# Four experts instead of three on the two-pass 64-slot step, and a new order of the 56 expert steps

## The reference

```python
logits = (xt @ w_router).astype(jnp.float32)
top_val, top_idx = lax.top_k(logits, TOP_K)          # 2 of 8 experts
top_w = jax.nn.softmax(top_val, axis=-1)
gates = jnp.sum(jax.nn.one_hot(top_idx, N_EXPERTS) * top_w[..., None], axis=1)
for e in range(N_EXPERTS):
    y = y + gates[:, e:e + 1] * (silu(xt @ w_gate[e]) * (xt @ w_up[e])) @ w_down[e]
```

## Time and profile before

| | |
|---|---|
| three runs, median | 1363.91 us |
| lowest and highest | 1363.8 and 1367.77 us |
| span of the profiled execution | 1365.5 us |
| PE busy in it | 1331.8 us, 98% |
| DVE busy | 1107.3 us, 81% |
| ScalarE busy | 975.5 us, 71% |
| moved by DMA | 433.24 MB, 317 GB/s on the mean |

### The profile page before, as it was taken

One profiled execution on the slowest core, in us unless ns is written; L12 is line 12 of the kernel. 1 busy time (PEld: TensorE's weight loads), 2 busy tenths in 40 slices (PEclk: granted clock), 3 DMA queues, 4 the chain that ended last, 5 costly groups with the idle time before them and its releaser, 6 DMA issues.

```text
span 1365.5 us, 18288 instructions
## 1 busy us (share of the span) xinstructions
PE 1331.8 (98%) x7233; PEld 1123.6 (82%) x7233; DVE 1107.3 (81%) x885; ACT 975.5 (71%) x930; POOL 168.7 (12%) x103
## 2 busy tenths in 40 slices
PE   8989999999999999999999999999999999999996
PEld 7888999999999778777877888777877877787784
DVE  4664655555666599999999989999999999999995
ACT  5465544446556667888788878888888888878883
POOL 4251000000000132574400000000000000000001
PEclk8999999999999999999999999999999999999998
DMA  9305755554542389999999999999999999999992
GB/s 372 121 1 185 207 186 184 184 184 154 204 144 86 111 332 401 404 419 407 412 421 419 421 401 390 422 421 421 408 411 421 414 411 421 421 411 422 418 418 98
DMA packets 67203, 433.24 MB, mean 317 GB/s; under 512 B 8160, under 2 KB 10336, under 8 KB 18992
## 3 DMA queue, kind: packets, MB, share of 16 engines
q1 hardware_dynamic: 60320, 418.01, 76.4%
q0 software_dynamic: 3360, 12.22, 3.0%
q10 hardware_dynamic: 3440, 1.91, 0.8%
HBM read 426.09 MB, written 6.03 MB: 316 GB/s over the span
## 4 chain that ended last, share of the span: by engine, by line
PE 74%; DVE 11%; DMA 9%; ACT 4%; issue 1%; SPq 0%; DVEq 0%; ACTq 0%
PE banks L1887 21%; PE banks L1889 20%; PE banks L1888 20%; DMA raw<-in_moe_w_gate 9%; DVE w_lo L1169 6%; ACT w_hi L623 2%; PE banks L2451 2%; DVE qk_lo L1169 2%; PE banks L2120 2%; PE banks L2452 2%; ACT qk_hi L623 1%; PE banks L2108 1%; PE banks L2488 1%; PE banks L2490 1%; PE banks L2462 1%
## 5 line engine op out<-in xcount | busy, mean ns | idle before, releaser
L1169 DVE TENSOR_TENSOR w_lo<-raw,w_hi 128x2048 fp32r<-128x2048 f32 (+1 forms) x312 | 711.2, 2297 | 134.4 <-ACT w_hi L623 132.9
L623 ACT CAST w_hi<-raw 128x2048 fp32r<-128x2048 f32 (+1 forms) x312 | 592.5, 1909 | 161.8 <-PE banks L1889 125.5
L1169 DVE TENSOR_TENSOR qk_lo<-raw,qk_hi 128x2048 fp32r<-128x2048 f32 x84 | 192.0, 2286 | 13.0 <-ACT qk_hi L623 12.1
L623 ACT CAST qk_hi<-raw 128x2048 fp32r<-128x2048 f32 x84 | 160.0, 1905 | 14.3 <-PE banks L1889 9.5
L1887 PE MATMUL banks<-w_hi,t_hi 128*128 128x512 f32 (+2 forms) x444 | 164.7, 371 | 2.9 <-DVE w_lo L1169 1.5
L1889 PE MATMUL banks<-w_lo,t_hi 128*128 128x512 f32 (+2 forms) x444 | 161.6, 364 | 0.0
L1888 PE MATMUL banks<-w_hi,t_lo 128*128 128x512 f32 (+2 forms) x444 | 161.5, 364 | 0.0
L1887 PE MATMUL banks<-t_hi,w_hi 128*128 128x256 f32 x544 | 155.5, 286 | 0.9 <-DVE t_lo L1190 0.9
L1888 PE MATMUL banks<-t_hi,w_lo 128*128 128x256 f32 x544 | 154.3, 284 | 0.0
L1889 PE MATMUL banks<-t_lo,w_hi 128*128 128x256 f32 x544 | 154.2, 284 | 0.0
L1887 PE MATMUL banks<-w_hi,h_hi 128*128 128x512 f32 x300 | 118.8, 396 | 0.2 <-DVE w_lo L1169 0.2
(11 more groups left out here) (358 smaller groups left out, 2261.9 us busy)
## 6 DMA issues: line engine op xcount, KB each, us to landing
raw<-in_moe_w_gate SPq DMA_DIRECT2D x112, 1024.0 KB, 9.9
raw<-in_moe_w_up SPq DMA_DIRECT2D x112, 1024.0 KB, 9.3
raw<-in_moe_w_down SPq DMA_DIRECT2D x112, 1024.0 KB, 9.7
raw<-in_na_w_qkv SPq DMA_DIRECT2D x12, 1024.0 KB, 4.8
raw<-in_ffn_w_gate SPq DMA_DIRECT2D x11, 1024.0 KB, 5.0
raw<-in_ffn_w_up SPq DMA_DIRECT2D x11, 1024.0 KB, 5.1
raw<-in_ffn_w_down SPq DMA_DIRECT2D x11, 1024.0 KB, 4.9
raw<-in_w_in_e SPq DMA_DIRECT2D x6, 1024.0 KB, 15.7
```

What stands on the lines that cost most here:

```text
L623: act.copy(tile_hi(u, n), raw[:, u.raw, 0:n]).then_inc(hi_done, 1)
L1169: dve.tensor_tensor(tile_lo(u, n), raw[:, u.raw, 0:n], tile_hi(u, n).bitcast(F32), ALU.subtract).then_inc(lo_done, 1)
```

## The change

The step kinds are dealt out anew: positions 1, 3, 5 and 6 are small instead of 1, 4 and 6, so there are 28 big and 28 small steps instead of 35 and 21. The order of the steps is given by a string, in which each letter takes the next step of its kind, instead of by a list of big steps with small ones put behind some of them. `RANK_OF` follows: the four experts with the fewest tokens are small. The threshold in the sort goes from 2.5 to 3.5 (`len(SMALL_V) - 0.5`). `TURN_AT`, `SENT_AT` and `MOVE_AT` are computed from the order as before.

```diff
 SMALL = 64
-BIG_V, SMALL_V = (0, 2, 3, 5, 7), (1, 4, 6)
-SMALL_AFTER = ((3, 4, 5, 6, 8, 9, 10), (15, 16, 17, 18, 20, 21, 22), (24, 25, 26, 27, 29, 30, 31))
-RANK_OF = np.array([7, 2, 3, 4, 1, 5, 0, 6], np.float32)
+BIG_V, SMALL_V = (0, 2, 4, 7), (1, 3, 5, 6)
+PATTERN = "BBBBSBSBSSBBSSSBBSSSBBSSBSBSBBSSBSSSBSSBBSBSSBSBBSSBSBBB"
+RANK_OF = np.array([7, 3, 4, 2, 5, 1, 0, 6], np.float32)

 def step_order():

-    order = []
-    for m in range(MOE_STEPS * len(BIG_V)):
-        order.append((BIG_V[m // MOE_STEPS], m % MOE_STEPS))
-        for v, after in zip(SMALL_V, SMALL_AFTER):
-            if m in after:
-                order.append((v, after.index(m)))
+    order, taken = [], {"B": 0, "S": 0}
+    for kind in PATTERN:
+        m = taken[kind]
+        order.append(((BIG_V if kind == "B" else SMALL_V)[m // MOE_STEPS], m % MOE_STEPS))
+        taken[kind] += 1
     return order
...
-                dve.tensor_scalar(extra, rank, 2.5, float(SLOTS - SMALL), ALU.is_lt, ALU.mult).then_inc(sort_step, 1)
+                dve.tensor_scalar(extra, rank, len(SMALL_V) - 0.5, float(SLOTS - SMALL), ALU.is_lt, ALU.mult).then_inc(sort_step, 1)
```

## The result

The kernel after takes 1369.76 us (median of 20 runs, 1366.72 to 1373.81), the kernel before, in 20 runs beside it, 1367.17 us (1362.91 to 1370.58). The ratio is 1.0023 [1.0014, 1.0033]: 3.1 us slower by the ratio. That is under the 0.3% which the prediction took for the limit of what can be told, but on the other side of no change than the forecast of -0.8 us, and outside its range. The runs of each kernel lie in two groups some 4 us apart (before 1362.9 to 1365.0 and 1367.1 to 1370.6, after 1366.7 to 1368.7 and 1370.8 to 1373.8), and both groups lie higher after.

What follows compares the result with a forecast made beforehand. Weight transfers were taken to bound the expert stage at about 421 GB/s, so PE's 33.6 us less work gave 0 us and the smaller add -0.8 us: 1363.1 us from a median of 1363.91, range 1359.5 to 1367.0.

Steps and rivals of the forecast that it cites:

- The bound: Expert stage: weight transfers, full at about 421 GB/s, set the pace; 33.6 us less PE work gains 0 us.
- PE was the bound: Rival, expert stage: PE sets the pace, so all 33.6 us go, giving 1330 us; chance 0.06.
- the tally: Expert stage: PE's 846 us against the queue's 861; big steps add 2.0 us of lateness, small ones take 2.8 away.
- PE's idle time: Small steps of the expert stage: about 34 us more PE idle time, waiting for w_lo.
- One add of 64 instead of 96 rows: Adding an expert's rows back: one more small add takes 0.8 us less from the weight queue, range 0.6 to 1.3.
- The new order up to the tally: Steps from 9 on: at most two big steps in a row behind step 4, three at the end; lateness stays covered.
- Queues that are moved past: POOL's adds and gathers at new steps: tightest is step 40, 0 us; the other place is a rival.
- the rival behind it: POOL late with expert 7's pick table at step 14: PE could wait 5.6 us, giving 1369 us; chance 0.05.
- The table of step 14: Sign of a wrong prediction: step 14 waits for expert 7's pick table, which could take 22.3 us.
- the cover: Four split tiles hold 10 us of PE's lateness before the ring of weight buffers stands still.
- If the granted clock leaves 1.00: Sign of a wrong prediction, in a run of small steps: at 1.2 GHz one takes up to twice 12.1 us.
- step 40: POOL's add of expert 5, 7.8 us, then gather of 7, 8.7 us (at most 14.4), fit two steps, 29.9 us: 0 us.

Runs made afterwards that it cites:

- the first kernel: Kernel before, with half of each down load left out in the expert stage (two of a step's six loads at half length): 1363.07 us, ratio 0.9966.
- the second: Kernel after with slot work of positions 5 to 7 one to three steps later, and half of each down load left out: 1338.24 us, ratio 0.9791 to before.
- the later slots: Kernel after with PE's and VectorE's slot work of positions 5 to 7 one to three steps later: ratio to before 0.9990, repeated 0.9991.
- the old head: Kernel after with steps 8 to 10 again small, big, small and the new order behind them: ratio to before 0.9998.
- the run with VectorE's wait: Kernel after with VectorE waiting in step 8 until POOL's pick table of position 5 is set: ratio to before 1.0003.

## Why the prediction was right or wrong

*The bound: right.* The quiet stretch at the end still moves 420 GB/s, latency is 10.3 to 10.6 us, ScalarE's waits went from PE to the DMA, and what was taken from PE was worth next to nothing while the loads stood. None of the stretches read above shows the 435 or 439 GB/s that the rival "PE was the bound" needed; and of that rival's 33 us, 24 came out by the ratio, and only when the loads were cut as well. (In the stage it is 28.2, 813.3 against 1296.33 - 511.23 = 785.1, or an estimated 22 without the first kernel's stop. In the second PE is busy 98% of 508 to 1296 us and VectorE holds 24% of the chain, so some of the relief may be hidden there again.) One term of the tally was off. PE does not stand 15 us under the queue: with the loads cut the kernel before still needed 813.3 us from gather to add (1322.77 - 509.44) against 811.7 with them, and without its stop and the slow clock an estimated 807.6, so PE is within some 4 us of the queue. What of PE's work the three windows of the earlier trace rows leave out was not added up.

*PE's idle time: right in kind, less in size.* Forecast 34 us more; the busy time in the stage fell by 25 (808.94 to 783.91; the part at half clock counts as busy, at most 3.4 of it), and 4.8 of the 25 are the stop. With the later slots, without the stop, it is 789.60, 19 us less than before. What the rest is was not looked into.

*One add of 64 instead of 96 rows: not contradicted.* -0.8 us forecast; the stages of the later slots, their repeat and the old head are 0.7, 0.6 and 0.7 us shorter, and the queue loses 0.8, 1.1 and 1.0 us less. That fits, but it hangs on one profile of the kernel before, and nothing in it separates the add from the rest of the change. The total of a run cannot show it (0.9990 [0.9977, 1.0003]).

*The new order up to the tally: right.* Old head, new rest costs nothing that shows.

*"Queues that are moved past", and the rival behind it: here it failed.* The mechanism was the right one (a late pick table on POOL, PE's slot matmuls waiting for it at the head of a step, all its matmuls behind them), and the rival's 1369 us came within a microsecond of the result. That nearness is luck: the rival's 5.6 us stood on a base of 1363.91 and at step 14, while the loss is 3.1 us on a base of 1367.17 and at step 10. The table of step 14, the text's sign of being wrong, kept nobody waiting. The place and the cover were wrong, and so was the chance of 0.05. Three steps of the working failed:

1. The text says that up to step 8 the order is the old one, and then looks at where adds and gathers have moved, and so at step 14. It did not ask of each slot step whether its margin holds. Steps 9 and 10 changed places, and the slot matmuls of position 5 stand between them. The margin could be had from before: the table ended at 628.8, PE came at 633.9, 5.1 us. On the axis of before (the first copy of the table is 4.54 us earlier in after) PE now comes at 631.9, 2.0 us earlier, behind a small step.
2. The duration of a table was taken as a number (22.3 us at the worst). It is a wait for something on VectorE. With the steps swapped it ends, on the same axis, at 636.5, 7.7 us later. 2.0 + 7.7 - 5.1 = 4.6 us are the 4.76 that PE stands. Within them lies the other wait, for the low parts of the turned rows, which grew from 1.01 to 2.2 us; the text does not name it.
3. The cover of 10 us needs four tiles that ScalarE can still write while PE stands, and a PE at its full clock behind the wait. Neither held: ScalarE wrote one tile and then waited 8.43 us. It had already been waiting for PE in that stretch, before as after (4.1 us in five places before; 3.1 us in five places after, beside the stop), so all tiles but one were taken when the stop came. And the clock fell. "If the granted clock leaves 1.00" stood among the signs of a wrong prediction, but for runs of small steps, not for a single stop.

*The base.* The forecast stood on a median of three runs, 1363.91; the 20 beside the kernel after have 1367.17. So 3.3 us of the 6.7 between 1363.1 and 1369.76 are the base, and the other 3.4 are the step above. That the three runs came out low was bad luck. The text also sets the profile's span of 1365.5 us against a median of times; in the record the time of a run is 1.8 to 2.1 us longer than its span, so that execution lay about 3.4 us above the median, not 1.6. The forecast, 1363.91 - 0.8, does not depend on it. At step 40 it takes the shortest landings of the earlier trace rows, 7.8 and 8.7 us, for the usual ones, which are 9.3 and 9.4; the two steps' room covers these too.

## What to carry to other kernels

When an order is changed, go along each engine's waits and not along the moved work: for each wait ask how early its releaser was (the margin in the trace of before) and how much earlier the waiting engine now comes; here a margin of 5 us met an arrival 2 us earlier and a release 8 us later. When two resources are both full, relief for one shows nothing, and a kernel that cuts the other tells whether the relief is there. Read the profile of such a kernel as well: here it had a stop of its own. A stop of PE can cost more than its length, if the clock falls with it and the buffers are already taken; here dummy matmuls in the stop gave back about half to two thirds of the loss, but only where they began ahead of the stop.

## What the runs showed of the hardware

POOL's pick operation (128 x 96, one input from SBUF) takes 0.52 us in a pause of VectorE. Beside VectorE's back-to-back subtracts it ended after 2.47 or 4.97 us in some places, and did not end for 19.18, 21.85, 29.58 or 38.72 us in others: many of VectorE's instructions long, not one. In the kernel before it ended within a pause of 0.32 us on VectorE, at 628.78; in after VectorE has no such pause from 602.4 to the end at 631.97. That a pause lets it end is shown by the run with VectorE's wait, where it took 0.53 us.

```profile
623.99 4.48 DVE L1169 TENSOR_TENSOR w_lo<-raw,w_hi 128x2048 fp32r<-128x2048 f32 x2
628.79 2.29 DVE L1169 TENSOR_TENSOR w_lo<-raw,w_hi 128x2048 fp32r<-128x2048 f32 x1 [0.32 <-ACT w_hi L623]
```

```profile
626.05 0.74 DVE L1793 SCALAR_TENSOR_TENSOR arena<-banks,arena 64x512 f32<-64x512 f32 x1
626.71 2.28 DVE L1168 TENSOR_TENSOR qk_lo<-raw,qk_hi 128x2048 fp32r<-128x2048 f32 x1
628.91 0.55 DVE L1820 TENSOR_TENSOR kc_rest<-banks,kc_rest 128x384 fp32r<-128x384 f32 x1
629.38 2.28 DVE L1168 TENSOR_TENSOR w_lo<-raw,w_hi 128x2048 fp32r<-128x2048 f32 x1
631.58 0.42 DVE L1800 TENSOR_TENSOR h_hi<-banks,h_hi 128x256 fp32r<-128x256 f32 x1
```

The subtracts of L1168 read both inputs from SBUF. The Trainium skill (SBUF — State Buffer, section Who interferes with whom) says that such an instruction contends with a GpSimd instruction that reads SBUF, and that an instruction with at most one input from SBUF, outside the modes that use both ports, does not. The first agrees with these rows. The second does so in part: in after the table ended during L1800 (one input from the PSUM banks), but not during L1793 or L1820 ahead of it, which are of the same kind, nor during an earlier L1800 at 616.91; an earlier table of the same profile did end during L1793, at 550.97. Why one lets POOL through and another not stays open.

Of TensorE's clock: in a stop of 4.76 us, and in one of 2.2 us in the kernel where the table was prompt, the granted clock went from 1.00 to 0.50 (2.4 to 1.2 GHz) and stayed there for 6.8 us, most of them with PE at work again; around the 1.01 us of the kernel before, and with dummy matmuls ahead of the waits, it stayed at 1.00. The length of a stop does not settle it alone. After's second profile has a stop of 2.21 us near 965 us, in which PE waits for a subtract of VectorE, and the clock stays at 1.00; in the first profile of the later slots the same wait is 1.97 us, and the clock is at 0.50 for 3.4 us behind it. What else decides stays open.

```profile
966.84 0.50 PE L2450 MATMUL banks<-qk_hi,t_hi 128*128 128x512 f32 x1 [2.21 <-DVE qk_lo L1168]
...
964.00:984.00 20.00, 16.60 (x72) 12.45 (x71) 18.93 (x10) 17.54 (x13) 0.00 (x0) 1.00 1.01 420
```
